# Attention's weighted sums of V as three fp32r products of high and low halves instead of one fp32 product

## The reference, cut to what matters

```python
logits = (jnp.einsum('bhqn,bhkn->bhqk', qb, kh).astype(jnp.float32) * scale
          + cqb[..., None] - ck[:, :, None, :])
logits = jnp.where(mask, logits, -jnp.inf)
p = jax.nn.softmax(logits, axis=-1)
return jnp.einsum('bhqk,bhkn->bhqn', p.astype(vh.dtype), vh)   # all float32
```

## Time and profile before

| | us |
|---|---|
| median of 3 runs (1923.52 to 1924.32) | 1924.19 |
| the profiled execution | 1921.38 |
| its span, first to last instruction | 1919.6 |
| TensorE busy in the span | 1836.2 (96%) |
| VectorE busy | 977.6 (51%) |
| ScalarE busy | 946.9 (49%) |
| GpSimd busy | 431.8 (22%) |

### The profile page before, as it was taken

How to read it: one execution, slowest core, us unless ns; L and a number is a source line. 1 busy time by engine, 2 the same in 40 slices (tenths; PEclk the granted TensorE clock), 3 DMA queues, 4 the chain that set the end, 5 groups by cost and what they waited for, 6 DMA issues and landing times.

```text
span 1919.6 us, 55790 instructions
## 1 busy us (share of the span) xinstructions
PE 1836.2 (96%) x24271; PEld 1596.3 (83%) x24271; DVE 977.6 (51%) x1873; ACT 946.9 (49%) x1712; POOL 431.8 (22%) x425
## 2 busy tenths in 40 slices
PE   6899999999999999999798999999999999999898
PEld 5798989898998989998698778888888888887676
DVE  7456665666666665666433652534344444344521
ACT  6455454545555554544323525364645555555621
POOL 2223142423323242421000321212121213111010
PEclk8999999999999999999799989999999999999899
DMA  6101010100101010101242110111111101111334
GB/s 234 45 11 45 6 52 9 45 16 28 31 19 42 6 52 9 52 9 30 85 147 103 46 34 16 35 29 28 29 28 29 38 24 39 28 29 28 99 100 136
DMA packets 103735, 89.85 MB, mean 47 GB/s; under 512 B 4101, under 2 KB 95864, under 8 KB 103240
## 3 DMA queue, kind: packets, MB, share of 16 engines
q1 hardware_dynamic: 99544, 66.41, 11.9%
q0 software_dynamic: 3168, 17.14, 2.8%
q10 hardware_dynamic: 784, 2.76, 0.4%
HBM read 64.96 MB, written 21.33 MB: 45 GB/s over the span
## 4 chain that ended last, share of the span: by engine, by line
PE 88%; DVE 5%; ACT 3%; issue 2%; DMA 1%; POOL 0%; SPq 0%; DVEq 0%; ACTq 0%; POOLq 0%
PE ps L1951 8%; PE ps L2563 7%; PE ps L1952 6%; PE ps L2460 6%; PE ps L1953 6%; PE ps L2461 6%; PE ps L2462 6%; PE ps L1877 3%; PE ps L2043 3%; PE ps L1879 3%; PE ps L1878 3%; PE ps L2062 3%; PE ps L2534 2%; PE ps L2506 2%; PE ps L2535 2%
## 5 line engine op out<-in xcount | busy, mean ns | idle before, releaser
L1951 PE MATMUL ps<-xh,wh 128*128 128x258 f32 (+1 forms) x1024 | 320.5, 313 | 4.1 <-ACT arena L1045 2.7
L1952 PE MATMUL ps<-xh,wl 128*128 128x258 f32 (+1 forms) x1024 | 291.6, 285 | 0.0
L1953 PE MATMUL ps<-xl,wh 128*128 128x258 f32 (+1 forms) x1024 | 291.1, 284 | 0.0
L2460 PE MATMUL ps<-xh,wh 128*128 128x348 f32 x744 | 254.5, 342 | 3.3 <-ACT arena_b L1305 3.3
L2461 PE MATMUL ps<-xh,wl 128*128 128x348 f32 x744 | 240.1, 323 | 0.0
L2462 PE MATMUL ps<-xl,wh 128*128 128x348 f32 x744 | 239.8, 322 | 0.0
L1822 DVE TENSOR_REDUCE arena_b<-ps 128x1 f32<-128x144 f32 (+4 forms) x224 | 106.2, 506 | 205.6 <-PE ps L2510 171.7
L1951 PEld LDWEIGHTS ps<-xh,wh 128*128 128x128 f32 x1024 | 193.8, 189 | 16.7 <-ACT arena L1045 4.6
L1952 PEld LDWEIGHTS ps<-xh,wl 128*128 128x128 f32 x1024 | 194.5, 190 | 1.9
L1953 PEld LDWEIGHTS ps<-xl,wh 128*128 128x128 f32 x1024 | 193.6, 189 | 0.0
L1014 ACT ACTIVATE arena<-ps,pp 128x257 f32<-128x257 f32 (+1 forms) x128 | 61.3, 479 | 227.2 <-PE ps L1953 227.2
(11 more groups left out here) (298 smaller groups left out, 4476.6 us busy)
## 6 DMA issues: line engine op xcount, KB each, us to landing
wr<-in_w_in SPq DMA_DIRECT2D x33, 512.0 KB, 4.5
xt_scr<-arena POOLq DMA_DIRECT2D x2, 4176.0 KB, 13.0
wr<-in_kv_w SPq DMA_DIRECT2D x16, 512.0 KB, 4.0
wr<-in_b_w_in SPq DMA_DIRECT2D x16, 512.0 KB, 3.9
arena<-xt_scr SPq DMA_DIRECT2D x8, 522.0 KB, 4.6
arena<-oa_scr SPq DMA_DIRECT2D x8, 520.0 KB, 4.5
wr<-in_w_out SPq DMA_DIRECT2D x8, 512.0 KB, 5.2
ob_scr<-arena_b POOLq DMA_DIRECT2D x16, 256.0 KB, 2.9
```

The lines of the kernel that those rows point to most:

```text
L1951: pe.matmul(bank, wh[:, j, k, :], xh[:, k, t], start=(k == 0), stop=False)
L1952: pe.matmul(bank, wl[:, j, k, :], xh[:, k, t], start=False, stop=False)
L1953: mm = pe.matmul(bank, wh[:, j, k, :], xl[:, k, t], start=False, stop=(k == KO - 1))
L2460: pe.matmul(bank[:, 0:SEG], wh[:, slot, k, :], xh[:, k, t], start=(k == 0), stop=False)
```

## The change

V and P are each written as a high half (rounded to fp32r) and a low half (the rest), and a unit's product is now three fp32r matmuls: high V by high P, low V by high P, high V by low P. ScalarE still writes the exponential, into `pt`, of which there are now two instead of four, and so waits for the low half two units back. After the exponentials of a group it makes the high halves by a copy, one for each unit. VectorE, at its step `scores`, subtracts high from `pt` for the low half. The halves of P have four buffers each, in the free slots of the weight tiles `wh` and `wl` (for the last head in other tiles). TensorE waits for the high half before the first product and for the low half before the third. For V, ScalarE evacuates the transposes to rows in `bsq`, and copies all 576 columns of a head to high V; VectorE subtracts for low V; the square that writes `bsq` waits for that. A number of semaphores of the forget gate are merged into two, and the tile `ones_r` with its memset goes.

```diff
-        vflat = [carve_b(NT * P).rearrange("p (t x) -> p t x", t=NT) for _ in range(2)]
-        pt = [carve_b(512) for _ in range(4)]
+        pt = [carve_b(512) for _ in range(2)]
...
+        def p_part(n_, low):
+
+            i = n_ % 4
+            if n_ // NU == 2 * KO - 1:
+                return p_last[low][i // 2][:, 512 * (i % 2):512 * (i % 2) + 512]
+            return p_store[low][:, 512 * i:512 * i + 512]
... ScalarE, square(p, j)
+                if p >= 0:
+                    act.wait_ge(S.v_lo, 2 * p + 2)
                 act.activation(bsq, (kb, qb)[j], ACT.Square).then_inc(S.hn_sq, 1)
... ScalarE, vrow
+                            act.wait_ge(S.b_evac, chunk(p, local) + 1)
+                            if p + e > 0:
+                                act.wait_ge(S.pv_done, NU * (2 * p + 1 - e))
+                            act.activation(vhi[:, :, v_cols(e)], rows_v, ACT.Copy).then_inc(S.v_hi, 1)
... ScalarE, scores
                             act.wait_ge(S.st_done, n_ + 1)
+                            if n_ >= 2:
+                                act.wait_ge(S.p_lo, n_ - 1)
+                            act.activation(pt[n_ % 2][0:n_k, 0:n_q], ps[0:n_k, B_ST[i], 0:n_q], ACT.Exp,
+                                           scale=SCALE).then_inc(S.p_exp, 1)
+                        for w in GROUPS[g]:
+                            n_k, _, n_q, _, _ = unit(w)
+                            n_ = NU * (2 * p + e) + w
+                            act.wait_ge(S.p_exp, n_ + 1)
                             if n_ >= 4:
                                 act.wait_ge(S.pv_done, n_ - 3)
-                            act.activation(pt[n_ % 4][0:n_k, 0:n_q], ps[0:n_k, B_ST[i], 0:n_q], ACT.Exp,
-                                           scale=SCALE).then_inc(S.p_exp, 1)
+                            act.activation(p_part(n_, 0)[0:n_k, 0:n_q], pt[n_ % 2][0:n_k, 0:n_q], ACT.Copy)\
+                                .then_inc(S.p_hi, 1)
... VectorE, new steps
+                    elif kind == "vrow" and st_[2]:
+                        e = st_[1]
+                        rows_v = v_rows.rearrange("p (t c) -> p t c", c=HD)
+                        dve.wait_ge(S.v_hi, 2 * (p + 1 - e) + e + 1)
+                        dve.tensor_tensor(vlo[:, :, v_cols(e)], rows_v, f32(vhi[:, :, v_cols(e)]),
+                                          ALU.subtract).then_inc(S.v_lo, 1)
+                    elif kind == "scores":
+                        e, g = st_[1:]
+                        for w in GROUPS[g]:
+                            n_k, _, n_q, _, _ = unit(w)
+                            n_ = NU * (2 * p + e) + w
+                            dve.wait_ge(S.p_hi, n_ + 1)
+                            dve.tensor_tensor(p_part(n_, 1)[0:n_k, 0:n_q], pt[n_ % 2][0:n_k, 0:n_q],
+                                              f32(p_part(n_, 0)[0:n_k, 0:n_q]), ALU.subtract).then_inc(S.p_lo, 1)
... TensorE, weighted
-                            pe.wait_ge(S.p_exp, n_ + 1)
+                            pe.wait_ge(S.p_hi, n_ + 1)
                             if w == 0:
-                                pe.wait_ge(S.b_evac, chunk(p - 1 + e, (L_VROW0, L_VROW1)[e]) + 2)
+                                pe.wait_ge(S.v_lo, 2 * p + e + 1)
...
-                            pe.matmul(ps[:, B_PV[qb_], q0 - 512 * qb_:512], vflat[e][0:n_k, kt, :],
-                                      pt[n_ % 4][0:n_k, 0:n_q], start=(kt == 0), stop=(kt == 4 * qb_ + 4),
+                            o = ps[:, B_PV[qb_], q0 - 512 * qb_:512]
+                            v_h, v_l = (a[0:n_k, kt, e * HD:e * HD + P] for a in (vhi, vlo))
+                            p_h, p_l = (p_part(n_, low)[0:n_k, 0:n_q] for low in (0, 1))
+                            pe.matmul(o, v_h, p_h, start=(kt == 0), stop=False, skip_group_check=True)
+                            pe.matmul(o, v_l, p_h, start=False, stop=False, skip_group_check=True)
+                            pe.wait_ge(S.p_lo, n_ + 1)
+                            pe.matmul(o, v_h, p_l, start=False, stop=(kt == 4 * qb_ + 4),
                                       skip_group_check=True).then_inc(S.pv_done, 1)
```

More of the change, by code:

```diff
@@ L210, in __init__ @@
         self.st_done = sem("st_done")
+        self.v_hi = sem("v_hi")
+        self.v_lo = sem("v_lo")
         self.p_exp = sem("p_exp")
+        self.p_hi = sem("p_hi")
+        self.p_lo = sem("p_lo")
         self.pv_done = sem("pv_done")
@@ L285, in build @@
         EXTRA = slice(HD, HD + 3)
-        ARENA_B = 13848
+        VB = 3 * HD
+        vhi, vlo = (sb(n, [P, NT, VB], F32R) for n in ("vhi", "vlo"))
+        ARENA_B = 10412
         arena_b = sb("arena_b", [P, ARENA_B])
@@ L396, in build, with v_cols @@
         NU = len(UNITS)
+        v_rows = bsq[:, 0:NT * HD]
+        def v_cols(e):
+            return slice(2 * e * HD, (2 * e + 1) * HD)
+        p_store = [a[:, 2:4, :, :].rearrange("p s k c -> p (s k c)") for a in (wh, wl)]
+        p_last = ((ka[0], qa[0]), (kb2[0], qb2[0]))
+        def p_part(n_, low):
[3 more added lines that the diff above has]
+            return p_store[low][:, 512 * i:512 * i + 512]
         def unit(w):
@@ L730, in _ @@
         def _(pool):
-            pool.memset(f32(ones_r[:, :]), 1.0).then_inc(S.setup_pool, 1)
+            pool.sem_inc(S.setup_pool, 1)
             pool.memset(head_ones[:, :], 0.0).then_inc(S.setup_pool, 1)
@@ L1260, in round_act @@
                     elif kind == "forget":
[L1261 to L1266, removed]
+                        act.wait_ge(S.f_step, 1)
+                        act.activation(f_a[0:H, :], f_in[0:H, :], ACT.Abs).then_inc(S.f_act, 1)
+                        act.wait_ge(S.f_act, 1)
+                        act.activation(f_a[0:H, :], f_a[0:H, :], ACT.Exp, scale=-1.0).then_inc(S.f_act, 1)
+                        act.wait_ge(S.f_act, 2)
+                        act.activation(f_a[0:H, :], f_a[0:H, :], ACT.Ln, bias=1.0).then_inc(S.f_act, 1)
                     elif kind == "forgotten":
-                        act.wait_ge(S.c_scaled, 1)
-                        act.activation(chi[0:H, :], f_b[0:H, :], ACT.Copy).then_inc(S.c_hi, 1)
+                        act.wait_ge(S.f_step, 5)
+                        act.activation(chi[0:H, :], f_b[0:H, :], ACT.Copy).then_inc(S.f_act, 1)
                     elif kind == "rsq":
@@ L1754, in _ @@
             g = G[N_F % 2]
-            dve.tensor_scalar(seg3(f_in[0:H, :]), g[0:H], fb_in[0:H, :], None, ALU.add).then_inc(S.f_logit, 1)
-            dve.memset(vflat[0][:, :, HD:], 1.0).then_inc(S.setup_b, 1)
-            dve.memset(vflat[1][:, :, 0:HD], 1.0).then_inc(S.setup_b, 1)
+            dve.tensor_scalar(seg3(f_in[0:H, :]), g[0:H], fb_in[0:H, :], None, ALU.add).then_inc(S.f_step, 1)
+            dve.memset(f32(vhi[:, :, HD:2 * HD]), 1.0).then_inc(S.setup_b, 1)
+            dve.memset(f32(vlo[:, :, HD:2 * HD]), 0.0).then_inc(S.setup_b, 1)
             dve.memset(f_b[0:H, :], 1.0).then_inc(S.setup_b, 1)
@@ L1777, in round_dve @@
                     elif kind == "forget":
-                        dve.wait_ge(S.f_logit, 1)
-                        dve.wait_ge(S.f_abs, 1)
+                        dve.wait_ge(S.f_step, 1)
+                        dve.wait_ge(S.f_act, 1)
                         dve.tensor_scalar(f_in[0:H, :], f_in[0:H, :], 0.0, None, ALU.min).then_inc(S.f_step, 1)
-                        dve.wait_ge(S.f_step, 1)
-                        dve.wait_ge(S.f_ln, 1)
+                        dve.wait_ge(S.f_step, 2)
```

38 lines of the change are left out of this document (15 added, 23 removed).

## The result

The median of four runs is 2047.28 us (2045.43 to 2048.84), against 1923.86 for the kernel before, measured beside it: ratio 1.0642 [1.0624, 1.0661]. Forecast were 2025, and 1985 to 2050 for the likeliest case. The profiled execution took 2048.84. The kernel is 123 us slower, with less to multiply than before.

The account below looks back on a forecast made before the run. TensorE, busy 89.39 of a round's 89.86 us, bounds the kernel. 1921.4 profiled + 70 for seven rounds + 12 for the last + 1 ahead + 18 for the clock = 2022; the runs' median lies 2.8 higher: 2025 us, range 1955 to 2075.

Parts of the forecast that it names:

- saved by the products: TensorE's three fp32r products in place of one fp32 product: 1.9 us less a round, 15 in all (13 to 25).
- weighted(1), e = 0: Surest stall: TensorE waits for group 1's low P, behind VectorE's stacks and GpSimd's hold on the port: 3.1 us a round.
- maxima in fill[3]: In e = 0, reductions come late behind added copies and subtractions; TensorE waits twice, 0.8 and 0.6 us.
- last of the maxima in fill[5]: In e = 0, TensorE waits for a reduction behind group 5's late copy and subtractions: 2.8 us (2.1 without the port).
- scores behind exponentials, e = 1: Group 1's exponentials come later by group 0's copies; TensorE waits before writing new scores: 1.1 us.
- weighted(1), e = 1: TensorE waits for group 1's low halves behind VectorE's lines 1803 and 1804: 2.2 plus 0.2, 2.4 us.
- V's evacuation: In fill[3] of e = 1, ScalarE's evacuation of V comes late by group 3's copies: 0.9 us.
- The sign that most of the idleness would be at group 1 of both heads: TensorE's idle time would stand ahead of the product with low P, most at group 1 of both heads; no size given.
- 12 drops of 3.4 us, 1.5 us each: 18: Long TensorE waits drop its clock to half for 3.4 us; 12 drops counted, 18 us in all (0 to 60).
- Rival (a): Half-idle engines deliver in time and the 15 us come in full: 1909 us; chance 0.05.
- Rival (b): Only the order bites: 5.0 us of waits a round less 1.9, no clock loss, 1950 us; chance 0.18 (1930 to 1985).
- (c): The clock falls twice in most rounds, costing 63 us in place of 18: 2070 us; chance 0.22 (above 2050).

Follow-up runs that it names:

- gpsimd_narrow: The changed kernel with GpSimd's two weight instructions cut to an eighth of their columns, order kept: 2003.52 us.
- products_only: The changed kernel without copies and subtractions for low halves; all three fp32r products take the same high halves: 1911.26 us.
- low_not_awaited: The changed kernel, VectorE still making low P, but the third product takes high P and does not wait for low P: 2031.45 us.
- copies_only: The changed kernel without VectorE's subtractions for low P; the third product takes high P, ScalarE's copies and V's halves stay: 1944.43 us.
- highs_placed: lows_behind_maxima with groups 6 and 7's low-P subtractions back right behind the scores, and group 3's high-P copies (e = 1) behind V's evacuation: 1962.07 us.
- rebuilt_order: lows_behind_maxima plus half a projection in fill[0], Z weights' high half behind group 1's exponentials, group 3's copies behind V's evacuation (both e = 1): 2026.18 us.
- lows_behind_maxima: The changed kernel with stacks and low Q's subtraction later, low-P products last in each group, low-P subtractions behind the filling's maxima: 2000.32 us.

## Why the forecast was right, and where not

The direction and the mechanism held: in-order queues deliver late at a few places, while the engines have room on average. Step by step:

| place | forecast, us a round | measured |
|---|---|---|
| saved by the products | 1.9 | 1.9 to 2.1 |
| weighted(0), e = 0 | none | 1.3 |
| weighted(1), e = 0 | 3.1 | 2.8 |
| maxima in fill[3] | 0.8 + 0.6 | 0.6 + 0.2 |
| last of the maxima in fill[5] | 2.8 | 2.2 |
| scores behind exponentials, e = 1 | 1.1 | 1.0 |
| weighted(1), e = 1 | 2.4 | 2.0 |
| V's evacuation | 0.9, and 0.5 of before | 1.4 |
| two reductions, e = 1 | 0.4 | none |

The waits of the kernel after sum to 11.6 in this round (from 1353.04; 11.4 in the mean) where 12.6 were forecast (12.1 and the 0.5). Most are within 0.6 of the forecast, and the one not foreseen stands against those that came out smaller. The wait at weighted(0) was missed since I had looked at GpSimd's line 879 only: it is line 766, the scaling, that holds the subtraction of 400 columns. The port itself was right: low P of unit 2 was forecast 1.4 us later by it, and gpsimd_narrow shows 44 us of the time to be its. The sign that most of the idleness would be at group 1 of both heads did not come: 2.8 and 2.0 of 11.6 stand there.

**The term that was mis-sized is the clock**, "12 drops of 3.4 us, 1.5 us each: 18". The mechanism is there, the size is not. The seven rounds are at half clock for 105.7 us where they were for 6.9, and the last round with the end for 24.6 where it was 13.9; 109.5 us more. Some 10 of these fall into waits, where no work is slowed; the other 99, at 45%, are 45 us. I had named three stalls of the size that costs clock in every round and then counted 12 drops for all rounds, less than two in each. In the round from 1353.04 there were 17 us: 6.8 at the wait of 2.81, and 3.4 each after those of 2.16, of 1.03 and 2.04, and of 1.40; in the next, with the same waits, 13.7.

The sum, by spans: 2047.0 - 1919.6 = 127.4. Ahead of the first round +4.3 (forecast 1). The seven rounds +115 (forecast 70 and nearly all of the 18): idle time in gaps over 50 ns 76.5 - 3.3 = 73, products -13, clock (98.8 - 6.4 in waits) x 0.45 = 42, and 14 behind the waits. Last round and end +8.2, its clock included (forecast 12 without).

The 14 was no term of the forecast. The first matmul after a wait has none before it to overlap with: the one of 400 columns at 1357.13 took 0.45 us, where in a stream it would have come 0.18 after its neighbour. Over a round's nine waits this makes 2.2 us by the records, against 0.3 for the one wait of the kernel before; 1.9 a round, 13 in seven, is nearly all of it. The ends of matmuls are modelled in the records, but the sum closes: a mean round less its idle time, less 45% of the half-clock time outside waits, less this term, is 87.0 to 87.6 us in all twelve kernels with three fp32r matmuls a unit, from products_only (87.96 long) to the kernel after (107.17).

So without the clock the seven rounds cost 73 where 70 were forecast, partly by luck: the waits alone came to less than forecast (73 for 85, before the savings), and the time behind them, which I had not counted, made up for it. By spans the forecast is 26 us short (22 by the medians, since I had added 2.8 for them): 27 for the clock (45 in place of 18), 3 each for the rounds and for the time ahead of them, less 7 for the last round.

The forecast named the product that waits for low P as its surest stall. That is where half of the idleness shows (6.2 of 11.6) but not what it hangs on: low_not_awaited takes that wait away and costs nearly as much. My expectations of the repairs were too low nearly every time (1999 for 2022, 1982 for 2004, 1974 for 2000, 1938 for 2026): I booked a removed wait as gained and did not ask what stands next in the queue. Rival (a), full gain, is what products_only shows. Rival (b) gave 1950, near copies_only's 1944, but by chance: its waits are those for low P, and copies_only has none of them. (c), with 63 us for the clock, was nearer in this one term (45) than the forecast.

The ladder in one line: products -13, ScalarE's copies and V's halves +33, VectorE's subtractions, with their hold on `pt`, +87, the wait for them at the product +16. Neither more buffers for `pt` nor low P on GpSimd was tried, and no version that makes and multiplies the low halves of P beat the kernel before.

## What to carry to other kernels

Where one engine is busy for 99% of a round, a step given to half-idle engines is priced by what stands behind it in their queues, not by their busy share: list, for each insertion, the next instruction on that engine that the full engine waits for, and its slack. Then look which other engine's instruction holds it by a shared port, and count every wait above a microsecond twice, for itself and for the clock that may follow, and 0.2 us more for the first matmul behind it. When a wait is taken away, find the next instruction in the same queue before booking the gain.

## What the runs showed of the hardware

- Means of a round: 11.4 us of idleness, in single waits of up to 2.8 us, went with 15.0 us at half clock (kernel after); 3.5 us with 2.0 (highs_placed); 7.1 with 17.8 (rebuilt_order). The idle sum does not tell the loss.
- A wait cost TensorE some 0.2 us beyond its idle time: nine waits in a round of the kernel after had first matmuls that took 2.2 us more than they would have added in a stream.
- Three fp32r products of 512 columns took 0.23 us each, 0.7 in all; the fp32 product they replace 0.86 (half of the 1.72 of a group of 512 + 512). One of 16 columns took 0.11, as much as one of 144.
- A VectorE subtraction with two SBUF operands of 144 columns took some 2.4 us while GpSimd had a long instruction of that kind, and one of 16 columns 1.9 (lows_behind_maxima). GpSimd's subtraction of 1024 columns (line 893) took 2.4 at the median and 2.8 at most in the kernel after.
